# Attention: the softmax scaling on GpSimd, and every second copy of the transposed probabilities on VectorE

## The chip, the cores and the metric

The kernel runs on one core of a Trainium2 chip. The metric is device time in microseconds of one execution. Three runs of the kernel before gave 2448.98, 2449.76 and 2450.52 us, median 2449.76 us.

## The reference

The program is a two-layer decoder trunk on 256 tokens of width 2048. Layer 0 mixes tokens with a diagonal state-space mixer, layer 1 with sparse attention, and each layer ends with a SwiGLU feed-forward part. The change touches only the core of the attention. For each of 16 heads of width 128, and each of two blocks of 128 queries, the reference does, with the 64 keys picked per query by a small indexer:

```
logits = einsum('bqhd,bqkhd->bhqk', qb, kg) * HEAD_DIM ** -0.5
logits = where(valid, logits, -inf)
p      = softmax(logits, axis=-1)
ob     = einsum('bhqk,bqkhd->bqhd', p, vg)
```

The kernel does not gather. It computes the logits against all keys of the block (128 for the first block of queries, 256 for the second) and adds a mask, `selb`, that is zero on the picked keys and very negative elsewhere.

## The kernel before

Each engine has its own program, in which instructions run in the order written; the engines meet at semaphores. Nearly all of the time is TensorE's: matrix products of float32 weights, each split in a high and a low part (line 2217), with the weights streamed from HBM by SyncE through a ring of four slots. ScalarE writes the high part (line 807) and VectorE the low part (line 1155). The weight splitting of the next product and the attention share these two engines one after the other.

The attention stands between the last projection ("v") and the output projection ("z", `attn_out`). Its unit is one head of one block of queries; there are 32, numbered a = 0 to 31. Heads 0 to 15 are *narrow* (128 keys), heads 16 to 31 *wide* (256 keys). Four engines work on them as a pipeline, written out by hand:

- TensorE, function `attention` in its program. Step a issues the logits of head a (line 2154, into `psA` or `psB`), then the transposition of head a-3 (line 2166, out of `prob` into `psT`), then the product of head a-4 with the values (line 2175, out of `probT` into `psM`; four heads fill one bank). The text calls the three L(a), T(a-3) and PV(a-4).
- VectorE. Step a makes the masked logits and their row minimum (line 1647, R(a)), the reciprocal of the row sum of head a-2 (line 1653, I(a-2)), and the scaling of that head's probabilities in place (line 1660, S(a-2)). Once in four steps, ahead of these, it writes the low part of four finished heads (line 1635, `o_lo`).
- ScalarE. Step a copies the transposed probabilities of head a-2 from PSUM to SBUF (line 1030, C(a-2)), then takes the exponential and row sum of head a (line 1036, E(a)), and once in four steps writes the high part of four finished heads (line 1042, `o_hi`).
- GpSimd does nothing in the attention. Its program goes through the same list of runs and, for the norm behind the attention, loads two chunks of layer-norm rows by DMA (line 740), which it issues before the attention begins.

Buffers: `prob` and `logit` have four slots by head modulo 4, `probT` and `psT` two by head modulo 2. The semaphores that order this are `lg_full` (L done), `lg_read` (R done), `exp_done` (E done), `p_ready` (S done), `pT_full` (T done), `pT_ready` (C done), `o_full`, `o_hi` and `o_ready`.

Of the kernel before, what the change touches and what calls it, by code (L numbers as in the profile page):

```python
# [34 lines left out]
P = 128  # L35
# [5 lines left out]
HEADS = 16  # L41
# [63 lines left out]
def build(nc, x, c, positions, ada_w, ada_b, ln_g, ln_b, s5_in_w, s5_a_re, s5_a_im, s5_log_dt, s5_b_re, s5_b_im,  # L105
          s5_c_re, s5_c_im, s5_d, s5_glu_w, s5_glu_b, dsa_in_w, dsa_out_w, ffn_w_in, ffn_w_out, consts, out):
    ctx = ExitStack()
    with ctx:
# [197 lines left out]
        gbias_landed, gate_ready, gate_full, gate_done = sem("gbias_landed"), sem("gate_ready"), sem("gate_full"), sem("gate_done")  # L306
        idx_full, idx_relu, idx_read = sem("idx_full"), sem("idx_relu"), sem("idx_read")
        key_raw, key_turned = sem("key_raw"), sem("key_turned")
        lg_read = sem("lg_read")
        lg_full, lg_ready, exp_done, p_ready, pT_full, pT_ready, o_full, o_hi, o_ready = (  # L310
            sem("lg_full"), sem("lg_ready"), sem("exp_done"), sem("p_ready"), sem("pT_full"), sem("pT_ready"),
            sem("o_full"), sem("o_hi"), sem("o_ready"))
# [402 lines left out]
        @block.gpsimd  # L715
        def _(pool):
            nc.gpsimd.memset(ident[:], 0.0).then_inc(const_ready, 1)
            nc.gpsimd.memset(ones[:].bitcast(F32), 1.0).then_inc(constants, 1)
            pool.wait_ge(const_ready, 1)
            nc.gpsimd.affine_select(out=ident[:], in_=ident[:], compare_op=ALU.not_equal, fill=1.0, base=0,  # L720
                                    pattern=[[-1, P]], channel_multiplier=1).then_inc(constants, 1)
            for ri in range(2):
                nc.gpsimd.memset(Bdiag[ri][:], 0.0).then_inc(constants, 1)

            def load_brow(q):
                chunk0, layer, c0, gate, _ = streamed(q)
                if gate is None:
                    return

                if q:  # L730
                    pool.wait_ge(chunk_stored, q)
                c0 += (q - chunk0) * AW
                pool.dma_start(brow[:], ada_b[layer:layer + 1, c0:c0 + AW].to_broadcast([P, AW])).then_inc(brow_landed, 16)

            def load_rows(norm, chunk):

                if 4 * norm + chunk >= 2:
                    pool.wait_ge(row_used, 4 * norm + chunk - 1)
                for which, src in ((0, ln_g), (1, ln_b)):
                    pool.dma_start(lnrow[:, chunk % 2, which],  # L740
                                   src[norm // 2, norm % 2:norm % 2 + 1, chunk * NB:(chunk + 1) * NB].to_broadcast([P, NB])
                                   ).then_inc(rows_landed[chunk % 2], 16)

            for r in runs:
                if r.before == "ln":
                    if r.norm == 0:
                        pool.wait_ge(w_lo_ready, rounded(r.unit + r.units - 1))
                    if r.norm == 2:
                        pool.wait_ge(idx_full, TOK * IDX_HEADS)
                    for chunk in range(4):  # L750
                        load_rows(r.norm, chunk)
                if r is glu:

                    pool.wait_ge(col_used, FRONT + 1)
                    for j in range(4):
                        pool.dma_start(gate_bias[32 * j:32 * j + 32], ada_b[0:1, 2 * D + j * NB:2 * D + (j + 1) * NB].to_broadcast([32, NB])
                                       ).then_inc(gbias_landed, 16)
                    pool.wait_ge(y_full, len(PIECES))
                if r.kind == "v":

                    pool.wait_ge(T_full, r.turn)
                    nc.gpsimd.memset(causal[:], 1.0).then_inc(const_ready, 1)
                    pool.wait_ge(const_ready, 2)
                    nc.gpsimd.affine_select(out=causal[:], in_=causal[:], compare_op=ALU.is_ge, fill=0.0, base=0,
                                            pattern=[[P, TOK], [-1, SEQ]], channel_multiplier=1).then_inc(constants, 1)
                if r.dense and r is not glu:
                    for q in range(r.dense[0], r.dense[0] + r.dense[1]):
                        load_brow(q)
                    continue
                if not r.ada and r is not glu:  # L770
                    continue
                for i in range(r.n):
                    q = chunk_of(r, i)
                    if r.kind == "glu":

                        pool.wait_ge(ps_free[1], r.use[1] + i)
                        for which, c0 in ((0, D), (1, 0)):
                            pool.dma_start(glub[:, which], s5_glu_b[0:1, c0 + i * NB:c0 + (i + 1) * NB].to_broadcast([P, NB])).then_inc(glub_landed, 16)
                    if q is not None:
                        load_brow(q)  # L780
                if r is glu:
                    for q in range(r.dense[0], r.dense[0] + r.dense[1]):
                        load_brow(q)

            pool.wait_ge(w_used, runs[-1].unit)
            for which, src in ((0, ln_g), (1, ln_b)):
                for chunk in range(4):
                    pool.dma_start(last_row[:, chunk, which],
                                   src[NORMS // 2, NORMS % 2:NORMS % 2 + 1, chunk * NB:(chunk + 1) * NB].to_broadcast([P, NB])
                                   ).then_inc(last_landed, 16)  # L790
# [3 lines left out]
        def _(act):  # L794
# [228 lines left out]
            def attention():  # L1023
                A = TOK * HEADS
                for a in range(A + 3):
                    if 2 <= a < A + 2:
                        b = a - 2
                        N = (b // HEADS + 1) * P
                        act.wait_ge(pT_full, b + 1)
                        nc.scalar.activation(probT[:, b % 2, 0:N], T[:, b % 2, 0:N], ACT.Copy).then_inc(pT_ready, 1)  # L1030
                    if a < A:
                        N = (a // HEADS + 1) * P
                        act.wait_ge(lg_read, a + 1)
                        if a >= 4:
                            act.wait_ge(pT_full, a - 3)
                        nc.scalar.activation(prob[a % 4][:, 0:N], logit[:, a % 4, 0:N], ACT.Exp, bias=soft[:, a % 4, 1:2], scale=-1.0,
                                             accum_out=soft[:, a % 4, 2:3]).then_inc(exp_done, 1)
                    if a >= 6 and a % 4 == 2:
                        g = (a - 6) // 4
                        t, h = divmod(4 * g, HEADS)  # L1040
                        act.wait_ge(o_full, g + 1)
                        nc.scalar.activation(hT_hi[:, h:h + 4, t * P:(t + 1) * P],
                                             M[:, g % 2].rearrange("p (h t) -> p h t", t=P), ACT.Copy).then_inc(o_hi, 1)
# [92 lines left out]
        def _(vec):  # L1136
# [491 lines left out]
            def attention():  # L1628
# [6 lines left out]
                    V.tensor_tensor(hT_lo[:, h:h + 4, t * P:(t + 1) * P], M[:, g % 2].rearrange("p (h t) -> p h t", t=P),  # L1635
                                    hT_hi[:, h:h + 4, t * P:(t + 1) * P].bitcast(F32), ALU.subtract).then_inc(o_ready, 1)

                for a in range(A + 2):
                    if a >= 9 and a % 4 == 1:
                        o_lo((a - 9) // 4)  # L1640
                    if a < A:
                        t = a // HEADS
                        N = (t + 1) * P
                        vec.wait_ge(lg_full, a + 1)
                        if a >= 4:
                            vec.wait_ge(exp_done, a - 3)
                        V.tensor_tensor_reduce(out=logit[:, a % 4, 0:N], in0=PS[a % 2][:, a // 2 % 2, 0:N],
                                               in1=selb[:, t, 0:N], scale=-HD ** -0.5, scalar=3.0e38, op0=ALU.add,
                                               op1=ALU.min, accum_out=soft[:, a % 4, 1:2]).then_inc(lg_read, 1)
                    if a >= 2:  # L1650
                        b = a - 2
                        vec.wait_ge(exp_done, b + 1)
                        V.reciprocal(soft[:, b % 4, 3:4], soft[:, b % 4, 2:3]).then_inc(dve, 1)
                        chain[0] += 1
                        inverse = chain[0]
                    if a >= 2:
                        b = a - 2
                        N = (b // HEADS + 1) * P
                        vec.wait_ge(dve, inverse)
                        V.tensor_scalar(prob[b % 4][:, 0:N], prob[b % 4][:, 0:N], soft[:, b % 4, 3:4], None, ALU.mult  # L1660
                                        ).then_inc(p_ready, 1)
                o_lo(A // 4 - 1)

            def finish(r, i, s):
# [107 lines left out]
        def _(pe):  # L1772
# [369 lines left out]
            def attention():  # L2142
# [14 lines left out]
                for a in range(A + 4):  # L2157
                    if a < A:
                        logits(a)
                    if 3 <= a < A + 3:  # L2160
                        b = a - 3
                        pe.wait_ge(p_ready, b + 1)
                        if b >= 2:
                            pe.wait_ge(pT_ready, b - 1)
                        for k in range(b // HEADS + 1):
                            ins = nc.tensor.transpose(T[:, b % 2, k * P:(k + 1) * P], prob[b % 4][:, k * P:(k + 1) * P], ident[:])
                        ins.then_inc(pT_full, 1)
                    if a >= 4:
                        b = a - 4
                        t, h = divmod(b, HEADS)  # L2170
                        pe.wait_ge(pT_ready, b + 1)
                        if b % 4 == 0 and b >= 8:
                            pe.wait_ge(o_ready, b // 4 - 1)
                        for k in range(t + 1):
# [145 lines left out]
```

## Time and profile before

| | us |
|---|---|
| median of three runs | 2449.76 |
| the profiled execution | 2452.9 |
| its span | 2451.2 |
| TensorE busy | 2391.7 (98% of the span) |
| VectorE busy | 1857.8 (76%) |
| ScalarE busy | 1042.6 (43%) |
| GpSimd busy | 35.3 (1%) |

The profiled execution is one run under the hardware profiler; its span is from the first to the last instruction. Times of rows are from the span's start. The attention runs from about 1580 to 1616 us of it, which is 1.5% of the span. All durations used below come from this execution.

### The profile page before, as it was taken

The numbers are of one execution on the slowest core, as the hardware profiler recorded it, in microseconds if no ns is written. First come the engines' busy times: TensorE is split into PE (matmuls) and PEld (weight loads), VectorE is DVE, ScalarE is ACT, GpSimd is POOL, SyncE is SP. The second block draws the span as 40 slices with busy tenths as digits, with TensorE's granted clock in tenths as the row PEclk, the third lists the DMA queues.
The fourth block names the chain that finished last, engine by engine and source line by source line (L and its number), as shares of the span: only waits on it lengthen the run. The fifth ranks groups of instructions, "written<-read, shape, count | busy, mean of one in ns | idle before, by whom it ended". The sixth has DMA issues, their size and how long they took to land.

```text
span 2451.2 us, 33454 instructions
## 1 busy us (share of the span) xinstructions
PE 2391.7 (98%) x12649; PEld 1923.6 (78%) x12649; DVE 1857.8 (76%) x2994; ACT 1042.6 (43%) x1245; POOL 35.3 (1%) x67
## 2 busy tenths in 40 slices
PE   7997899999999999999999999999999999999998
PEld 5584578878888888888878888778888888888886
DVE  8469969878878887898878987887777754455457
ACT  5353123464434444344454344555544334443442
POOL 0000000000000000000000000000000000000000
PEclk9998999999999999999999999999999999999999
DMA  9978748779989997898758877646788666666674
GB/s 376 398 253 314 285 166 310 248 230 344 311 284 310 341 306 264 292 331 299 254 167 291 290 250 228 203 138 191 254 293 288 220 196 189 189 189 191 195 218 144
DMA packets 311664, 627.39 MB, mean 256 GB/s; under 512 B 26608, under 2 KB 27024, under 8 KB 311504
## 3 DMA queue, kind: packets, MB, share of 16 engines
q1 hardware_dynamic: 306576, 611.27, 73.9%
q0 software_dynamic: 4288, 13.90, 2.0%
q8 instruction: 102, 1.67, 0.3%
q14 instruction: 58, 0.48, 0.1%
q10 hardware_dynamic: 640, 0.08, 0.0%
HBM read 623.05 MB, written 2.10 MB: 255 GB/s over the span
## 4 chain that ended last, share of the span: by engine, by line
PE 94%; DVE 2%; DMA 2%; ACT 1%; issue 1%; SPq 0%; DVEq 0%; ACTq 0%
PE psB L2217 42%; PE psA L2217 41%; DMA col_raw<-in_ada_w 2%; PE psT L1783 1%; PE psM L1815 1%; PE psA L2049 1%; PE psM L1826 1%; PE psT L2030 1%; PE psB L2030 0%; PE psT L1847 0%; PE psT L2019 0%; PE psA L2005 0%; PE psM L1796 0%; PE psM L1795 0%; DMA biasn<-in_ada_b 0%
## 5 line engine op out<-in xcount | busy, mean ns | idle before, releaser
L1155 DVE TENSOR_TENSOR w_lo<-w_raw,w_hi 128x1024 fp32r<-128x1024 f32 x732 | 893.1, 1223 | 465.5 <-ACT w_hi L807 461.0
L807 ACT ACTIVATE w_hi<-w_raw 128x1024 fp32r<-128x1024 f32 x732 | 774.8, 1060 | 1093.5 <-PE psB L2217 497.6
L2217 PE MATMUL psB<-w_hi,hT_hi 128*128 128x512 f32 x1040 | 407.3, 392 | 0.0
L2217 PE MATMUL psB<-w_hi,hT_lo 128*128 128x512 f32 x1040 | 404.9, 389 | 0.0
L2217 PE MATMUL psB<-w_lo,hT_hi 128*128 128x512 f32 x1040 | 404.7, 389 | 0.0
L2217 PE MATMUL psA<-w_hi,hT_hi 128*128 128x512 f32 x1008 | 397.6, 394 | 2.4 <-DVE w_lo L1155 2.1
L2217 PE MATMUL psA<-w_hi,hT_lo 128*128 128x512 f32 x1008 | 392.9, 390 | 0.0
L2217 PE MATMUL psA<-w_lo,hT_hi 128*128 128x512 f32 x1008 | 392.4, 389 | 0.0
L1172 DVE SCALAR_TENSOR_TENSOR ada_acc<-ada_raw,csil,ada_acc 128x512 f32<-128x512 f32 x465 | 347.5, 747 | 14.3 <-DVE ada_acc L1172 0.9
L2217 PEld LDWEIGHTS psB<-w_hi,hT_hi 128*128 128x128 f32 x1040 | 195.2, 188 | 45.9 <-issue 4.5
L2217 PEld LDWEIGHTS psA<-w_hi,hT_hi 128*128 128x128 f32 x1008 | 189.2, 188 | 49.1 <-issue 8.0
L2217 PEld LDWEIGHTS psB<-w_hi,hT_lo 128*128 128x128 f32 x1040 | 195.2, 188 | 40.8
L2217 PEld LDWEIGHTS psB<-w_lo,hT_hi 128*128 128x128 f32 x1040 | 195.3, 188 | 40.0
L2217 PEld LDWEIGHTS psA<-w_hi,hT_lo 128*128 128x128 f32 x1008 | 189.2, 188 | 40.0
L2217 PEld LDWEIGHTS psA<-w_lo,hT_hi 128*128 128x128 f32 x1008 | 189.4, 188 | 37.8
L2217 PE MATMUL psA<-w_hi,aT_hi 128*128 128x512 f32 x448 | 175.0, 391 | 0.8 <-DVE aT_lo L1712 0.7
L2217 PE MATMUL psA<-w_hi,aT_lo 128*128 128x512 f32 x448 | 174.4, 389 | 0.0
L2217 PE MATMUL psA<-w_lo,aT_hi 128*128 128x512 f32 x448 | 174.3, 389 | 0.0
L2217 PE MATMUL psB<-w_hi,aT_hi 128*128 128x512 f32 x432 | 169.1, 391 | 0.0
L2217 PE MATMUL psB<-w_hi,aT_lo 128*128 128x512 f32 x432 | 168.1, 389 | 0.0
L2217 PE MATMUL psB<-w_lo,aT_hi 128*128 128x512 f32 x432 | 168.1, 389 | 0.0
L2217 PEld LDWEIGHTS psA<-w_hi,aT_hi 128*128 128x128 f32 x448 | 84.1, 188 | 18.7 <-issue 1.6
(376 smaller groups left out, 2316.8 us busy)
## 6 DMA issues: line engine op xcount, KB each, us to landing
w_raw<-in_ffn_w_in SPq DMA_DIRECT2D x352, 512.0 KB, 4.6
ada_raw<-in_ada_w SPq DMA_DIRECT2D x496, 256.0 KB, 5.5
w_raw<-in_ffn_w_out SPq DMA_DIRECT2D x176, 512.0 KB, 4.7
col_raw<-in_ada_w SPq DMA_DIRECT2D x128, 512.0 KB, 7.4
w_raw<-in_dsa_in_w SPq DMA_DIRECT2D x112, 512.0 KB, 4.6
w_raw<-in_s_glu_w SPq DMA_DIRECT2D x56, 512.0 KB, 5.7
w_raw<-in_s_in_w SPq DMA_DIRECT2D x32, 512.0 KB, 7.8
w_raw<-in_dsa_out_w SPq DMA_DIRECT2D x32, 512.0 KB, 5.0
```

The costliest lines, as they stand in the source:

```text
L807: nc.scalar.activation(high(u), w_raw[:, u % RING], ACT.Copy).then_inc(w_hi_ready, 1)
L1155: V.tensor_tensor(low(u), w_raw[:, u % RING], high(u).bitcast(F32), ALU.subtract).then_inc(w_lo_ready, 1)
L1172: V.scalar_tensor_tensor(out=ada_sum(q), in0=ada_tile(q, k), scalar=csil[:, k:k + 1], in1=ada_sum(q), op0=ALU.mult, op1=ALU.add).then_inc( ...
L1783: ins = nc.tensor.transpose(T[:, j // 2, (j % 2) * SEQ + t * P:(j % 2) * SEQ + (t + 1) * P], src(t, j), ident[:])
L1815: ins = MM(M[row:row + 32, 0], csil[:, k:k + 1].to_broadcast([P, 32]), col_tile(a + w)[:, b * NB:(b + 1) * NB], start=k == 0, stop=k == AU ...
L1826: ins = MM(M[row:row + 32, v % 2], csil[:, k:k + 1].to_broadcast([P, 32]), col_tile(a + half)[:, b * NB:(b + 1) * NB], start=k == 0, stop= ...
L2030: ins = MM(outputs_place(n, f, d)[rows], Ctab[d][ri][:, f, rows], st[:, c0:c0 + HALF, half, g, ri, f % 8], start=False, stop=f % 4 == 3 an ...
L2049: ins = MM(PS[0][:, t], uT[:, kt, tok], glu_raw[k][:, kk], start=kt == 0, stop=kt == KT - 1)
L2217: ins = MM(PS[s][:, t, 0:r.width], a_[:, kt, tok], b_[:, kk, 0:r.width], start=kt == begin and m == 0, stop=kt == (end or r.units * UK) - ...
```

## The change

The scaling moves from VectorE to GpSimd, which runs it for all 32 heads in order, each behind a new semaphore `inverse_ready` that the reciprocal raises. The loop stands in GpSimd's program at the attention's place, so ahead of the two chunks of layer-norm rows for the norm behind it. ScalarE keeps the copies of even heads. The copies of odd heads move to VectorE, with a semaphore of their own, `pT_other`; VectorE makes the copy of head a-4 at the end of its odd step a, and its loop is two steps longer.

```diff
+                if r.before == "attention":
+                    for b in range(TOK * HEADS):
+                        N = (b // HEADS + 1) * P
+                        pool.wait_ge(inverse_ready, b + 1)
+                        nc.gpsimd.tensor_scalar(prob[b % 4][:, 0:N], prob[b % 4][:, 0:N], soft[:, b % 4, 3:4], None, ALU.mult
+                                                ).then_inc(p_ready, 1)
...
-                    if 2 <= a < A + 2:
+                    if 2 <= a < A + 2 and a % 2 == 0:
                         b = a - 2
                         N = (b // HEADS + 1) * P
                         act.wait_ge(pT_full, b + 1)
...
-                for a in range(A + 2):
+                for a in range(A + 4):
...
-                    if a >= 2:
+                    if 2 <= a < A + 2:
                         b = a - 2
                         vec.wait_ge(exp_done, b + 1)
-                        V.reciprocal(soft[:, b % 4, 3:4], soft[:, b % 4, 2:3]).then_inc(dve, 1)
-                        chain[0] += 1
-                        inverse = chain[0]
-                    if a >= 2:
-                        b = a - 2
+                        V.reciprocal(soft[:, b % 4, 3:4], soft[:, b % 4, 2:3]).then_inc(inverse_ready, 1)
+                    if a >= 4 and a % 2:
+                        b = a - 4
                         N = (b // HEADS + 1) * P
-                        vec.wait_ge(dve, inverse)
-                        V.tensor_scalar(prob[b % 4][:, 0:N], prob[b % 4][:, 0:N], soft[:, b % 4, 3:4], None, ALU.mult
-                                        ).then_inc(p_ready, 1)
+                        vec.wait_ge(pT_full, b + 1)
+                        V.tensor_copy(probT[:, b % 2, 0:N], T[:, b % 2, 0:N]).then_inc(pT_other, 1)
...
-                            pe.wait_ge(pT_ready, b - 1)
+                            pe.wait_ge((pT_ready, pT_other)[b % 2], b // 2)
...
-                        pe.wait_ge(pT_ready, b + 1)
+                        pe.wait_ge((pT_ready, pT_other)[b % 2], b // 2 + 1)
```

## Rows read from the trace of the kernel before

**Rows 1.** Stretches of the span: length; us busy of PE, PEld, DVE, ACT, POOL, granted TensorE clock, DMA share, GB/s.
```profile
1580.40:1593.30 12.90, 10.04 (x70) 8.42 (x71) 10.78 (x62) 10.39 (x44) 0.00 (x0) 1.00 0.32 114
1593.30:1616.00 22.70, 21.40 (x142) 16.48 (x141) 17.69 (x77) 17.50 (x61) 0.00 (x0) 1.00 0.00 1
1616.00:1650.00 34.00, 34.00 (x151) 28.11 (x151) 28.52 (x32) 14.28 (x14) 0.00 (x0) 1.00 0.66 217
```

**Rows 2.** Chain of waits, narrow heads: start us, us on the chain, what.
```profile
1585.07 0.29 DVE logit L1647
...
1585.51 0.30 DVE prob L1660
1585.85 0.33 PE psT L2166
...
1586.66 0.29 DVE logit L1647
```

**Rows 3.** TensorE in order of time, narrow heads: start us, us, line, operation, operands.
```profile
1586.02 0.39 PE L2175 MATMUL psM<-probT,v 128*128 128x128 f32 x2
1586.24 0.39 PE L2154 MATMUL psA<-qkT 128*128 128x128 f32 x2
1586.46 0.32 PE L2166 MATMUL psT<-ident,prob 128*128 128x128 f32 x1
...
1589.36 0.32 PE L2166 MATMUL psT<-ident,prob 128*128 128x128 f32 x1
...
1592.86 0.32 PE L2166 MATMUL psT<-ident,prob 128*128 128x128 f32 x1
```

**Rows 4.** TensorE in order of time, wide heads.
```profile
1596.51 0.60 PE L2154 MATMUL psB<-qkT 128*128 128x256 f32 x2
...
1601.14 0.60 PE L2154 MATMUL psB<-qkT 128*128 128x256 f32 x2
1601.57 0.38 PE L2166 MATMUL psT<-ident,prob 128*128 128x128 f32 x2
1601.79 0.61 PE L2175 MATMUL psM<-probT,v 128*128 128x128 f32 x4
1602.24 0.60 PE L2154 MATMUL psA<-qkT 128*128 128x256 f32 x2
...
1606.38 0.38 PE L2166 MATMUL psT<-ident,prob 128*128 128x128 f32 x2
```

**Rows 5.** VectorE in order of time, one low part and one wide head.
```profile
1587.39 0.69 DVE L1635 TENSOR_TENSOR hT_lo<-psM,hT_hi 128x512 fp32r<-128x512 f32 x1
1588.00 0.28 DVE L1647 CUSTOM_DVE_ANT_0 logit<-psB,selb 128x128 f32<-128x128 f32 x1
...
1597.14 0.42 DVE L1647 CUSTOM_DVE_ANT_0 logit<-psB,selb 128x256 f32<-128x256 f32 x1 [0.27 <-PE psB L2154]
...
1597.49 0.16 DVE L1653 RECIPROCAL soft<-soft 128x1 f32<-128x1 f32 x1
1597.69 0.35 DVE L1660 TENSOR_SCALAR prob<-prob,soft 128x256 f32<-128x256 f32 x1
```

**Rows 6.** VectorE groups by shape: a copy out of PSUM, count, busy us, mean ns.
```profile
L1516 DVE COPY st<-psM 128x512 f32<-128x512 f32 x4 | 2.6, 688 | 1.4 <-PE psM L2005 1.4
```

**Rows 7.** GpSimd in order of time: its computing instructions.
```profile
1.24 0.29 POOL L720 TENSOR_SCALAR_AFFINE_SELECT ident<-ident 128x128 f32<-128x128 f32 x1
1.48 1.79 POOL L723 MEMSET Bdiag_re<- 128x2048 f32 x1
...
1493.64 0.62 POOL L764 TENSOR_SCALAR_AFFINE_SELECT causal<-causal 128x512 f32<-128x512 f32 x1
```

**Rows 8.** All engines in order of time: GpSimd woken by VectorE.
```profile
1797.11 0.68 DVE L1188 SCALAR_TENSOR_TENSOR grow<-psM,brow 128x512 f32<-128x512 f32 x1
...
1798.09 0.54 POOL L733 DMA_DIRECT2D brow<-in_ada_b  x1 [52.38 <-DVE grow L1188]
```

**Rows 9.** A stretch with a lower granted clock, columns as in rows 1.
```profile
220.00:230.00 10.00, 5.04 (x32) 0.83 (x32) 10.00 (x65) 0.00 (x0) 0.00 (x0) 0.76 1.02 411
```

More of the change, by code:

```diff
@@ L308, in build @@
         key_raw, key_turned = sem("key_raw"), sem("key_turned")
-        lg_read = sem("lg_read")
+        lg_read, inverse_ready, pT_other = sem("lg_read"), sem("inverse_ready"), sem("pT_other")
         lg_full, lg_ready, exp_done, p_ready, pT_full, pT_ready, o_full, o_hi, o_ready = (
```

## The prediction

> **What bounds the kernel now.** I read the table of stretches first. Behind the attention TensorE is busy for the whole of the stretch [rows 1], so what the attention gives or takes moves the end of the span one for one: no later stage waits on something else that could absorb it. In the attention itself TensorE is busy 10.04 of 12.90 us with narrow heads and 21.40 of 22.70 us with wide ones [rows 1]. The reader is to see that there is little to win with wide heads and a little more with narrow ones.
>
> Then I read the chain of waits in the narrow part. It goes round once in two heads: R(a) at 1585.07, S(a-2) 0.44 later, T(a-2) 0.34 after that, L(a+2) 0.39 after T, and R(a+2) 0.42 after L, which is 1585.07 to 1586.66, 1.59 us [rows 2, 3]. Once in four heads o_lo holds VectorE for 0.61 us [rows 5], and four heads take 3.50 us (1589.36 to 1592.86) [rows 3]. Wide heads take 4.81 us for four (1601.57 to 1606.38) [rows 4].
>
> **The pieces that I use**, start to start. Narrow: L 0.22 [rows 3]; T 0.17 (1585.85 to 1586.02) and PV 0.22 [rows 2, 3]; L to R 0.42; R to I 0.24 (0.44 less the 0.20 from I to S in the wide rows) [rows 2, 3, 5]. Wide: L 0.43, T 0.22, PV 0.45 [rows 4]; L to R 0.63 (1596.51 to 1597.14), R to I 0.35, I to the next instruction 0.20 [rows 4, 5]. An instruction's end to its waiter's start costs 0.05: the scaling lasts 0.29 and T starts 0.34 after it [rows 2].
>
> **The change part by part.**
>
> *The scaling off VectorE.* Removed: 32 instructions that took 0.21 to 0.28 of VectorE's line. On the chain above I to T was 0.20 + 0.34 = 0.54. It becomes the reciprocal's 0.16 [rows 5] plus X, X being the way into GpSimd, the multiplication there, and the way to TensorE. No row shows this multiplication on GpSimd. The nearest is its select of the same kind (one tensor in, one out): 0.29 for 128 columns and 0.62 for 512, so about 0.40 for 256 [rows 7]. The longest computing row is 1.79 [rows 7]. The way in is 0.05 at the least, and 0.30 by the row in which a VectorE result (ends 1797.79) releases a DMA issue at 1798.09 [rows 8]. I take the select: X = 0.05 + 0.29 + 0.05 = 0.39 narrow and 0.50 wide. The lower end is the same less a third. For the upper end I take 1.79 for wide and half, 0.90, for narrow, with 0.30 on the way in: X = 1.25 and 2.14.
>
> GpSimd's select took 0.33 us for 384 more columns, 0.86 ns each [rows 7]. The Trainium skill, "GPSIMD Engine Reference", section 3.1, speaks against this part of the change: elementwise work belongs on VectorE, since GpSimd needs about 2.6 cycles of 1.2 GHz per element. By that the multiplication would be, as an estimate, 0.28 and 0.55 plus the dispatch, and X some 0.1 to 0.3 larger than mine; the sum below would be the same, as the limits on X there show. The trace has the one-input select well under that rate; for the multiplication itself no row decides.
>
> *The copy of odd heads to VectorE.* This is where I see the cost. VectorE makes C(a-4) at the end of its odd step a, behind R(a) and I(a-2). R(a) needs L(a). TensorE issues L(a), T(a-3) and then PV(a-4), which needs this very copy. So PV(a-4) cannot start until L(a) has gone through VectorE, and everything of TensorE queues behind PV(a-4): L(a+1) and T(a-2) above all. ScalarE's copy was made right after T(a-4), some two steps earlier. The copy reads PSUM: 128x512 took 0.69 [rows 6]; R, which also reads PSUM, took 0.28 for 128 and 0.42 for 256 [rows 5]; I take 0.29 and 0.42, the bounds being the scaling's 0.35 and the copy's 0.69, worth -0.07 and +0.27 a pair.
>
> A pair of narrow heads, a odd, from L(a) = 0: R 0.42, I 0.66, copy 0.86, PV(a-4) 0.86 + 0.29 + 0.05 = 1.20, L(a+1) 1.42, T(a-2) 1.64, PV(a-3) 1.81 (ScalarE's copy was done long before), L(a+2) 2.03. Against it, once in four heads: I(a-1) falls at 1.42 + 0.42 + 0.24 = 2.08, o_lo at 2.28, and R(a+2) at 2.89 where it was due at 2.45, so 0.44 more. Four heads: 2 x 2.03 + 0.44 = 4.50 against 3.50.
>
> A pair of wide heads: R 0.63, I 0.98, copy 1.18, PV(a-4) 1.65, L(a+1) 2.10, T(a-2) 2.53, PV(a-3) 2.75, L(a+2) 3.20. o_lo ends at 3.28 + 0.61 = 3.89 where R(a+2) was due at 3.83: 0.06. Four heads: 6.46 against 4.81.
>
> *Is X covered?* T(a-1) follows L(a+2) and stands just ahead of PV(a-2), which cannot start before 2.03 + 1.20 = 3.23. T may start as late as 3.06 and cost nothing; its reciprocal ends at 2.08 + 0.16 = 2.24. So X is free up to 0.82 narrow. Wide: 3.20 + 1.65 - 0.22 = 4.63, less 3.24, so up to 1.39. My 0.39 and 0.50 are covered by the wait for the copy. Without that cover a pair costs 1.21 + X narrow, 1.81 + X wide (the loop of rows 2 with X in it).
>
> *The copy off ScalarE.* Sixteen copies fewer. ScalarE is not the last to arrive any more, so this is worth nothing.
>
> *The moved loads.* Four DMA issues of GpSimd for layer-norm rows go behind its 32 multiplications. The norm is beyond the 34 us of products shown [rows 1], an issue took 0.54 [rows 8], so nothing waits. If they were late, it would cost about 2 us.
>
> **The sum.** Start of the pipeline, the first transposition through GpSimd with nothing to hide it: 0.2. Heads 4 to 16, twelve narrow steps: 3 x 1.00 = 3.0. Heads 16 to 20, logits wide and copies narrow, the mean of the two: (1.00 + 1.65) / 2 = 1.3. Heads 20 to 31, eleven steps of 1.65 / 4 = 0.41: 4.5. The tail behind L(31): the last o_lo but one, I(31), C(29) and then C(31) follow each other on VectorE, where S(31) alone was late: about 0.9, with an error of as much. Together 9.9 us. The profiled execution would go from 2452.9 to 2462.8; the median of the runs is 3.1 below it, so 2449.8 + 9.9 = 2459.7.
>
> **Rivals.**
>
> *GpSimd is dear.* Same mechanism, but X beyond the limits, so T and not PV comes last. With the upper end: narrow 2.46 a pair against 1.75, six pairs, 4.3; wide 3.95 against 2.41, seven and a half pairs, 11.6; start and tail 1.1. Together 17.0, 2466.8. For it: no row shows the operation. Against: three compute rows of GpSimd at under 1 ns a column.
>
> *Relief wins (faster).* VectorE's line is the busiest after TensorE's, o_lo's 0.61 shows on the chain, and it loses 0.2 to 0.3 a head. If the copies of odd heads came early enough, TensorE would go at its own pace: narrow 0.61 a head, 3.50 - 2.44 = 1.06 in four, times 3; wide 1.10 a head, 4.81 - 4.40 = 0.41 in four, times 3.75. That is 3.2 + 1.5 = 4.7, 2445.1. The point that decides is whether C(a-4) starts before L(a) does; by the order written it starts 0.86 after. Only if TensorE ran L(a) well ahead of PV(a-4), against that order, would it be so.
>
> *It evens out.* The added wait is as long as the time that VectorE's line is freed by, the multiplications saved giving back the rest: 2450. For it: the cost falls on every second head only. Against: the pair comes to 2.03 against 1.75 with VectorE's relief already in it.
>
> *The clock falls.* Where TensorE was busy 5.04 of 10 us the granted clock was 0.76 [rows 9], the mean of 2.4 and 1.2 GHz; at 10.04 of 12.90 it stayed at 1.00 [rows 1]. After the change the narrow part has 1.22 us of issues in 2.25. If the clock fell to 1.2 GHz through four wide pairs, about 2.0 of TensorE's work on each pair's loop would double, 8 us, and some 2 us more at the start of the products: 9.9 + 10 = 2469.7. Against: the gaps stay under 1 us.
>
> **How the numbers follow.** The forecast as worked out, 2457 to 2462, has 0.68. Dear GpSimd, 2462 to 2467 or above, 0.15. The clock 0.04. Relief 0.07. Evening out 0.06. About 0.2%, 4.9 us, is what a measurement of this kernel can tell from no change. Slower by more is 0.68 + 0.15 + 0.04 = 0.87, within 0.06, faster 0.07: relief's 4.7 is at the edge, and I count it as faster. The range is 2456.5 to 2467.0: it takes in the dear end of X, and the cheap end of the copy together with a tail that costs nothing; the clock, relief and evening out stay outside.
>
> **What would show it.** In the changed trace the chain of waits should pass from L to R, I and the new copy on VectorE and from there to PV, in every odd head. TensorE should idle before PV of odd heads by about 0.8 us narrow and 1.0 wide, put down to VectorE's `probT`, and hardly before T. Four heads should take 4.5 and 6.5 us, and the attention 45 us where it took 35. GpSimd's multiplication should last 0.3 to 0.6. I am wrong if TensorE's idle time stands before T and names GpSimd's `prob`, if GpSimd's instructions take over 0.8, or if PV of odd heads starts less than 1 us after L of four heads on.

## The result, and the profile after

The changed kernel takes 2461.38 us (median of 6 runs, 2460.27 to 2461.85) against 2450.03 us for the kernel before (6 runs): 11.35 us more, ratio 1.0044, 95% interval [1.0034, 1.0054]. It is slower, by 9.9 us in the forecast and by 11.35 in the measurement, and inside the range of 2456.5 to 2467.0.

The two profiled spans differ by less, 2459.5 against 2451.2 us. The attention began at 1577.05 in the one and at 1580.38 in the other, although all that had changed ahead of it were four DMA issues of GpSimd for layer-norm rows, which now come behind it; the profiled execution of the kernel before had lost some 3 us earlier on. Had the moved loads won these 3 us, the medians would differ by some 8 us and not by 11.35. So from here on the measure is the *length* of the attention, from the first logits to the first product behind it: 35.37 us before (1580.38 to 1615.75), 46.85 us after (1577.05 to 1623.90), 11.48 more.

The table of stretches, after (narrow heads, wide heads, the products behind; columns as in [rows 1]):

```profile
1577.05:1594.97 17.92, 13.17 (x69) 10.59 (x70) 8.65 (x56) 9.42 (x38) 8.23 (x14) 0.81 0.23 79
1594.97:1623.90 28.93, 23.30 (x141) 16.82 (x140) 14.46 (x65) 14.59 (x51) 17.54 (x22) 1.00 0.01 2
1623.90:1658.00 34.10, 34.10 (x153) 28.25 (x152) 28.23 (x32) 14.28 (x14) 0.66 (x2) 1.00 0.74 246
```

VectorE's busy time in the narrow part fell from 10.78 to 8.65 us and ScalarE's from 10.39 to 9.42 [rows 1], and yet the part is 5 us longer: work was taken from engines, and time was added between them. Behind the attention TensorE is busy throughout, as before, so the delay stays. The third number to read is the clock, 0.81 in the narrow part where it had been 1.00.

TensorE in order of time, wide heads of the changed kernel, the counterpart of [rows 4]:

```profile
1608.17 0.60 PE L2157 MATMUL psB<-qkT 128*128 128x256 f32 x2
1609.29 0.44 PE L2169 MATMUL psT<-ident,prob 128*128 128x128 f32 x2 [0.52 <-POOL prob L763]
1609.69 0.71 PE L2178 MATMUL psM<-probT,v 128*128 128x128 f32 x4
1610.24 0.60 PE L2157 MATMUL psA<-qkT 128*128 128x256 f32 x2
1610.67 0.38 PE L2169 MATMUL psT<-ident,prob 128*128 128x128 f32 x2
1610.89 0.61 PE L2178 MATMUL psM<-probT,v 128*128 128x128 f32 x4
1611.34 0.60 PE L2157 MATMUL psB<-qkT 128*128 128x256 f32 x2
```

A pair takes 3.17 us (L at 1608.17 to L at 1611.34), where 3.20 was forecast. PV of the odd head starts 1.52 after L (1608.17 to 1609.69), 1.65 was forecast. VectorE and GpSimd between the two, the counterparts of [rows 5] and [rows 7]:

```profile
1608.81 0.42 DVE L1653 CUSTOM_DVE_ANT_0 logit<-psB,selb 128x256 f32<-128x256 f32 x1
...
1609.15 0.16 DVE L1659 RECIPROCAL soft<-soft 128x1 f32<-128x1 f32 x1
1609.23 0.41 DVE L1664 COPY probT<-psT 128x256 f32<-128x256 f32 x1
```

```profile
1596.21 0.60 POOL L763 TENSOR_SCALAR prob<-prob,soft 128x128 f32<-128x128 f32 x1 [1.10 <-DVE soft L1659]
...
1608.31 0.92 POOL L763 TENSOR_SCALAR prob<-prob,soft 128x256 f32<-128x256 f32 x1 [1.14 <-DVE soft L1659]
```

The copy ends at 1609.64 and PV starts 0.05 later. GpSimd's multiplication ends at 1609.23 and T starts at 1609.29. From T to PV it takes 0.27 when T comes after a wait and PV does not (1600.01 to 1600.28), so by T alone PV could have gone at 1609.56: the copy is last, by 0.13 us. Multiplications take 0.60 and 0.92, where the nearest rows of GpSimd had suggested 0.29 and 0.40.

The waits of the attention, after (engine, tile and line, for whom: us in all, times, longest):

```profile
PEld psT L2169 <- POOL prob L763: 14.6, 19, 1.7
PE psT L2169 <- POOL prob L763: 9.0, 14, 1.5
PEld psM L2178 <- DVE probT L1664: 4.0, 13, 0.7
PE psM L2178 <- DVE probT L1664: 0.9, 3, 0.5
```

Most of these waits carry GpSimd's name, and so does the chain of waits (the counterpart of [rows 2]):

```profile
1607.71 0.31 DVE logit L1653
1608.06 0.08 DVE soft L1653
1608.14 0.09 DVE soft L1659
1608.23 0.08 issue
1608.31 0.93 POOL prob L763
1609.24 0.04 issue
1609.29 0.44 PE psT L2169 x2
1609.72 0.68 PE psM L2178 x4
1610.40 0.45 PE psA L2157 x2
```

Read alone, this chain says that GpSimd is the cause. The ends of two waits lie 0.13 us apart here, and the profile shows TensorE idle only before the first of them. Which one counts is for the experiments.

Stretch by stretch, from one transposition to another, before and after, in us:

| | before | after | more |
|---|---|---|---|
| first L to T(0) | 2.28 | 2.67 | 0.39 |
| T(0) to T(4) | 3.19 | 5.11 | 1.92 |
| T(4) to T(8) | 3.51 | 5.12 | 1.61 |
| T(8) to T(12) | 3.50 | 4.63 | 1.13 |
| T(12) to T(16) | 4.08 | 5.43 | 1.35 |
| T(16) to T(20) | 4.63 | 6.11 | 1.48 |
| T(20) to T(24) | 4.81 | 6.33 | 1.52 |
| T(24) to T(28) | 4.82 | 6.34 | 1.52 |
| T(28) to the product | 4.55 | 5.11 | 0.56 |

### The profile page after: what moved, and what is told of

Same layout as the page of the kernel before. It is cut to its first block, busy times and chain, and to the rows that moved or that the text cites. A ratio compares the mean times of both kernels' runs of the same rounds, so it can differ in the third digit from the quotient of the medians.

```text
span 2459.5 us, 33454 instructions
## 1 busy us (share of the span) xinstructions
PE 2396.7 (97%) x12649; PEld 1926.0 (78%) x12649; DVE 1852.3 (75%) x2978; ACT 1038.6 (42%) x1229; POOL 59.6 (2%) x99
## 4 chain that ended last, share of the span: by engine, by line
PE 88%; DVE 8%; DMA 1%; ACT 1%; issue 1%; POOL 0%; SPq 0%; DVEq 0%; ACTq 0%
PE psB L2220 41%; PE psA L2220 39%; DVE prod L1497 2%; DVE tmp L1502 1%; DVE st L1508 1%; PE psT L1786 1%; PE psM L1818 1%; DVE w_lo L1161 1%; DMA w_raw<-in_dsa_out_w 0%; DMA w_raw<-in_s_in_w 0%; PE psA L2052 0%; POOL prob L763 0%; PE psM L2178 0%; PE psT L1850 0%; PE psT L2033 0%
```

## The experiments

Two theories. *A*: VectorE's late copy holds PV of odd heads behind L, R and I of the same step, and GpSimd is hidden behind that. *B*: GpSimd's multiplication, late into TensorE, sets the time. *C* is about the clock and comes last. Results first, as a map ("narrow" is T(8) to T(12), "wide" T(20) to T(24); low clock is the time at 1.2 GHz by the granted clock in 2 us stretches):

| kernel | length | narrow | wide | low clock | median of the runs |
|---|---|---|---|---|---|
| before | 35.37 | 3.50 | 4.81 | none | 2450.0 |
| the change | 46.85 | 4.63 | 6.33 | 6.8 | 2461.4 |
| e1 scaling alone | 42.29 | 3.93 | 5.87 | none | 2457.5 |
| e2 late copy alone | 53.84 | 6.68 | 7.44 | 13.6 | 2472.1 |
| e3 change, copy early | 43.45 | 4.17 | 5.87 | 3.4 | 2458.9 |
| e4 change, half of GpSimd's columns | 45.71 | 4.48 | 6.33 | 6.8 | 2460.4 |
| e5 before, one step deeper | 32.05 | 3.05 | 4.40 | 3.4 | 2446.1 |
| e6 early copy alone | 38.41 | 3.70 | 5.14 | 3.4 | 2452.4 |
| e7 change, idle stretch filled | 46.04 | 5.12 | 6.34 | 3.4 | 2460.5 |
| e8 change, early and deeper | 33.75 | 3.26 | 4.39 | 3.4 | 2449.0 |
| e9 change, late and deeper | 44.79 | 4.51 | 6.33 | 6.8 | 2459.4 |

In e2 the whole narrow stretch, and in e7 1.5 us of it, lie at the low clock, so these two figures are not to be compared with the rest of their column. The kernel before, run beside them, had medians of 2450.64 us with e1 to e4, 2450.95 with e5 to e8 and 2450.98 with e9.

### e1: the scaling on GpSimd alone

```diff
 (in the changed kernel)
-                    if 2 <= a < A + 2 and a % 2 == 0:
+                    if 2 <= a < A + 2:
 ...
-                    if a >= 4 and a % 2:
-                        b = a - 4
-                        ...
-                        V.tensor_copy(probT[:, b % 2, 0:N], T[:, b % 2, 0:N]).then_inc(pT_other, 1)
 ...
-                        pe.wait_ge((pT_ready, pT_other)[b % 2], b // 2 + 1)
+                        pe.wait_ge(pT_ready, b + 1)
```

> The scaling on GpSimd alone; ScalarE makes all copies. Length of the attention, from the first logits to the first product behind it: 35.4 us before, 46.9 after the whole change. Theory A (the late copy on VectorE holds PV of odd heads, and GpSimd's 0.60 and 0.92 us are mostly hidden behind it): without that copy nothing hides GpSimd, a pair costs 1.21 + 0.73 = 1.94 narrow and 1.81 + 1.06 = 2.87 wide against 1.75 and 2.41, so about 6 us over before: length 41.5, time 2456. Theory B (GpSimd's multiplication sets the time, the copy matters little): the whole cost stays, length 46 to 47, time 2461.

Length 42.29, median 2457.54 us, ratio 1.0029 [1.0018, 1.0039]. Theory A's 41.5 is near, B's 46 to 47 is not. The chain of waits, wide heads:

```profile
1605.51 0.45 PE psA L2152 x2
1605.96 0.02 issue
1605.98 0.06 DVE logit L1653
1606.04 0.29 issue
1606.33 0.08 DVE soft L1653
1606.41 0.09 DVE soft L1659
1606.50 0.08 issue
1606.58 0.93 POOL prob L763
1607.51 0.04 issue
1607.56 0.44 PE psT L2164 x2
```

Here the loop really runs L, R, I, multiplication, T, and a pair costs 2.93 us (5.87 / 2), where 1.81 + X with X = 1.06 gave 2.87. GpSimd by itself costs 6.9 us of length (42.29 against 35.37). It is shorter than the change's 6.33 for four wide heads, so this loop is not what bounds the change.

### e2: the late copy alone

```diff
 (in the changed kernel; the loop on GpSimd is gone)
-                        V.reciprocal(soft[:, b % 4, 3:4], soft[:, b % 4, 2:3]).then_inc(inverse_ready, 1)
+                        V.reciprocal(soft[:, b % 4, 3:4], soft[:, b % 4, 2:3]).then_inc(dve, 1)
+                        ...
+                        V.tensor_scalar(prob[b % 4][:, 0:N], prob[b % 4][:, 0:N], soft[:, b % 4, 3:4], None, ALU.mult
+                                        ).then_inc(p_ready, 1)
```

> The odd copies on VectorE alone, at the same place; the scaling stays on VectorE between reciprocal and copy. Theory A: the copy now stands behind R, I and S, 0.12 (narrow) to 0.25 us (wide) and the wait between I and S later than in the whole change; about 14 us over before, more than the whole change: length 49, time 2463 to 2464. Theory B: near before, length 36 to 37, time 2451.

Length 53.84, median 2472.09 us, ratio 1.0085 [1.0070, 1.0100]. With no work on GpSimd at all it is the slowest of all: B falls here. Theory A has the sign, but its length of 49 is too small by 5 us and its time by 8. Part of this is the clock: 13.6 us at 1.2 GHz are in its profile. As 3.4 us of them cost 0.7 to 0.8 us in two pairs of profiles below, 13.6 would be worth some 3, an estimate; the rest stays open.

### e3: the change with the copy one step earlier

```diff
-                    if a >= 4 and a % 2:
-                        b = a - 4
+                    if 4 <= a < A + 4 and a % 2 == 0:
+                        b = a - 3
```

> The whole change with VectorE's copy of an odd head one step earlier, at the end of step a-1, so ahead of R(a) and its wait for L(a). Theory A: PV no longer waits for the copy, what is left is the loop through GpSimd, about 7 us over before: length 42.5, time 2457, and TensorE waits for GpSimd's prob alone. Theory B: no change against the whole change, length 46 to 47, time 2461.

Length 43.45, median 2458.85 us, ratio 1.0031 [1.0020, 1.0043], a little over what A said. Wide heads take 5.87 for four, as in e1: with the copy out of the way, what is left is the loop through GpSimd. So the early copy by itself gives back only 3.4 of the 11.5 us; the second loop stands close behind the first.

### e4: GpSimd scales half the columns

Half of each head's probabilities stays unscaled.

```diff
-                        N = (b // HEADS + 1) * P
+                        N = (b // HEADS + 1) * P // 2
                         pool.wait_ge(inverse_ready, b + 1)
```

> The whole change with GpSimd scaling only the first half of each head's columns (the other half stays unscaled), so about 0.45 us narrow and 0.60 wide. Theory A: T moves earlier but PV does not, at most 0.1 us a pair narrow and nothing wide: length 45 to 46, time 2460. Theory B: 0.15 us a pair narrow and 0.32 wide come back, with a little at the ends 3.5 to 4 us: length 43, time 2457.5.

Length 45.71, median 2460.38 us, ratio 1.0038 [1.0025, 1.0051]. TensorE, wide heads:

```profile
1607.98 0.60 PE L2157 MATMUL psB<-qkT 128*128 128x256 f32 x2
1608.78 0.44 PE L2169 MATMUL psT<-ident,prob 128*128 128x128 f32 x2 [0.20 <-POOL prob L763]
1609.50 0.71 PE L2178 MATMUL psM<-probT,v 128*128 128x128 f32 x4 [0.28 <-DVE probT L1664]
```

The multiplication fell from 0.92 to 0.60 us, and the wait before T from 0.52 to 0.20, exactly as much. The 0.32 us come back as a wait of 0.28 before PV; PV is 1.52 after L as before, and four wide heads take 6.33 as before. The wait that the profile put down to GpSimd was worth nothing in the wide part. In the narrow part it was worth 0.15 in four heads (4.63 to 4.48), and over the whole attention 1.14 us (46.85 to 45.71), within what A allowed and far from B's 43.

### e9 and e8: the loop through GpSimd spread over three heads

Both are the changed kernel with one step more between the logits and the rest: TensorE transposes head a-4 and multiplies head a-5 at step a, and ScalarE's copies, o_hi and o_lo follow one step later. They differ in VectorE's copy alone:

```diff
 (TensorE, in both)
-                    if 3 <= a < A + 3:
-                        b = a - 3
+                    if 4 <= a < A + 4:
+                        b = a - 4
 ...
-                    if a >= 4:
-                        b = a - 4
+                    if a >= 5:
+                        b = a - 5
 (VectorE's copy, e8)
+                    if a >= 5 and a % 2:
+                        b = a - 4
 (VectorE's copy, e9)
+                    if a >= 6 and a % 2 == 0:
+                        b = a - 5
```

> As e8_deep_both, but VectorE's copy behind R(a) and I(a-2) of the step in which TensorE needs it, as in the change; the loop through GpSimd stays spread over three heads. Theory A: PV of odd heads waits again for L(a), R(a), I(a-2) and the copy, 1.04 to 1.10 us narrow and about 1.5 wide behind L(a): 8 to 9 us over e8, length 41.5 to 42.5, time 2456 to 2458. Theory B (only the loop through GpSimd mattered, the place of the copy does not): as e8, length 34, time 2449.

> The whole change (scaling on GpSimd, odd copies on VectorE) with one step more between logits and transposition, and the copies ahead of R(a). Theory A: the loop through GpSimd is spread over three heads, 1.94 / 3 = 0.65 and 2.87 / 3 = 0.96 a head, below TensorE's own 1.10 for wide heads; nothing of the change's cost is left and 2 to 3 us are won over before: length 32.5 to 33.5, time 2447.5 to 2448.5. Theory B (GpSimd is too slow for its share, 0.93 us a wide head): length above 38.

e9: length 44.79, median 2459.38 us, ratio 1.0036 [1.0021, 1.0050]. Its length is 2.3 us over the upper end of what A said, with 6.8 us at 1.2 GHz in it. TensorE, wide heads:

```profile
1604.86 0.60 PE L2157 MATMUL psA<-qkT 128*128 128x256 f32 x2
1605.30 0.38 PE L2169 MATMUL psT<-ident,prob 128*128 128x128 f32 x2
1606.38 0.71 PE L2178 MATMUL psM<-probT,v 128*128 128x128 f32 x4 [0.70 <-DVE probT L1664]
1606.93 0.60 PE L2157 MATMUL psB<-qkT 128*128 128x256 f32 x2
```

T does not wait at all in these heads now, GpSimd is out of the picture there, and PV starts 1.52 us after L once more. Four wide heads take 6.33, the same as the change; the 2.06 us of length between e9 and the change lie elsewhere. e8, where only the copy's place is another, takes 4.39: 1.94 us in four heads for one line's position. Its length is 33.75 and its median 2449.04 us, ratio 0.9992 [0.9983, 1.0001], which cannot be told from the kernel before; A had said 32.5 to 33.5, and 2 to 3 us under the kernel before, which the medians do not show. The same instructions on the same engines as in the change cost nothing against the kernel before, though e5, with the same depth and neither part of the change, is 1.70 us shorter still.

### e6: the early copy alone

e2 with the copy placed as in e3.

> Scaling on VectorE as before; VectorE makes the odd copies at the end of step a-1, ahead of R(a). Against e2 (the same copies one half step later, length 53.8) it moves only the place. Theory A: the place was the cost: about 1.5 to 2.5 us over before, from the copy's own 0.2 to 0.35 us on VectorE: length 37 to 38, time 2452 to 2453. Rival (VectorE simply has too much work with the copies): length above 45.

Length 38.41, median 2452.35 us, ratio 1.0005 [0.9996, 1.0014], within 0.5 us of A's upper end of 38 and far from the rival's 45. From e2 to e6, 15.4 us of length go with the copy's place; VectorE has the same work in both.

### e5: the kernel before, one step deeper

```diff
 (in the kernel before; ScalarE, then TensorE)
-                    if 2 <= a < A + 2:
-                        b = a - 2
+                    if 3 <= a < A + 3:
+                        b = a - 3
 ...
-                    if 3 <= a < A + 3:
-                        b = a - 3
+                    if 4 <= a < A + 4:
+                        b = a - 4
 ...
```

PV, o_hi and o_lo follow one step later as well.

> The kernel before with one step more between the logits and the rest: TensorE transposes head a-4 and multiplies head a-5 at step a, ScalarE copies head a-3; nothing on GpSimd, no copy on VectorE. Theory A (the attention before and after the change is bound by loops of latencies: L, R, I, S, T, and back to L two heads later): the loop is spread over three heads, and the engines' own work is left, 0.77 narrow (VectorE) and 1.10 wide (TensorE) a head against 0.875 and 1.20, so 3 to 4.5 us less than before: length 31 to 32.5, time 2446 to 2447.5. Rival: VectorE or ScalarE is already the bound and a longer pipeline only lengthens the tail: length 35.5 to 36.5, time 2450 to 2451.

Length 32.05, median 2446.10 us, ratio 0.9979 [0.9970, 0.9988]: 4.9 us faster than the kernel before, and the fastest of all. Its chain of waits, wide heads, stays on TensorE, which is the bound there:

```profile
1600.07 0.43 PE psB L2154 x2
1600.50 0.22 PE psT L2166 x2
1600.72 0.45 PE psM L2175 x4
1601.17 0.43 PE psA L2154 x2
```

1.10 us a head is TensorE's own time, and 4.40 in four heads is what was measured. So the kernel before was held by a loop of latencies over two heads, and not by an engine. The scaling on GpSimd put more latency into that loop (e1). The late copy made a second one beside it, from L(a) to PV(a-4) within one step of TensorE, and that one a deeper pipeline does not loosen (e9).

### e7, e10 and e11: the clock

The granted clock in the changed kernel's first microseconds (columns as in [rows 1]):

```profile
1578.00:1579.00 1.00, 0.18 (x2) 0.00 (x0) 0.66 (x8) 0.99 (x5) 0.00 (x0) 1.00 0.87 262
1579.00:1580.00 1.00, 0.28 (x2) 0.28 (x3) 0.32 (x3) 0.14 (x2) 0.94 (x2) 0.76 0.95 356
1580.00:1581.00 1.00, 1.00 (x6) 0.92 (x6) 0.34 (x3) 0.76 (x4) 0.25 (x1) 0.50 0.95 367
...
1586.00:1587.00 1.00, 1.00 (x8) 0.91 (x7) 0.42 (x4) 0.78 (x2) 0.00 (x0) 0.83 0.02 8
```

0.50 is 1.2 GHz. Theory C: the idle stretch of 1.54 us before the first transposition, longer than before by 0.39, brought it on. e7 fills it:

```diff
                     if a < A:
                         logits(a)
+                    if a == 3:
+                        for _ in range(7):
+                            MM(M[:, 1, 0:P], ident[:], ident[:], start=True, stop=True)
```

> The whole change with seven products of the identity with itself (128x128, about 0.22 us each, into a bank of psM that the first later products overwrite) between the first four logits and the first transposition, where TensorE sat idle for 1.5 us. Theory C (that idle stretch lets the clock fall to 1.2 GHz for the 6.5 us behind it, and this costs 1.5 us or more of the 46.9): the granted clock stays at 1.00, length 45 to 45.5, time 2459.5 to 2460. Rival (the clock does not hang on this stretch, since the same stretch stood at full clock with the scaling alone on GpSimd): the clock falls all the same in this or another place, length 46 to 47, time 2461.

Length 46.04, median 2460.51 us, ratio 1.0039 [1.0025, 1.0053]. The seven products fill the stretch from 1577.92 to 1579.63, and T(0) comes 2.68 after the first logits, as in the change. The clock still fell, later (1586.6 to 1590.0) and for 3.4 us. e1 had the same start as the change, T(0) 2.67 after the first logits, and kept 1.00. Two unchanged kernels were profiled again:

> The kernel before, profiled once more. Theory C (only kernels with longer idle stretches of TensorE lose the clock in the attention): granted clock 1.00 through the attention, length 35.4. Rival (it is a matter of the single execution): 0.95 or less in the attention and a length of 36 to 37.

> The changed kernel, profiled once more. Theory C: the clock falls again at the start of the attention, length 46 to 47. Rival: the clock falls elsewhere or not at all, and the length differs with it, 45 to 46 at full clock.

The kernel before, second profile: length 36.04, and a low clock that its first profile had not shown:

```profile
1582.00:1584.00 2.00, 2.00 (x10) 1.95 (x11) 1.32 (x8) 1.52 (x8) 0.00 (x0) 0.53 0.55 212
1584.00:1586.00 2.00, 2.00 (x12) 1.83 (x10) 1.27 (x8) 1.18 (x6) 0.00 (x0) 0.61 0.00 0
```

The changed kernel, second profile: length 46.85, the clock low again, from about 1578.6 to 1585.5. So C falls as stated: the low clock comes in the attention of the kernel before as well, in some executions. What differs is how long it lasts, 3.4 us there and 6.8 in the change, and e7's single profile does not settle why. What starts it was not found.

## Why the prediction was right, and where it was off

**Nothing behind absorbs it.** Right: TensorE is busy 34.10 of 34.10 us behind the attention, and 11.48 us of length are 11.35 us of median.

**The copy holds PV of odd heads.** Right for wide heads, and shown from three sides: e2 has the late copy without GpSimd, e4 halves GpSimd's time and the wide heads do not move, e9 takes GpSimd out of the loop and keeps 6.33. Forecast were 4.50 and 6.46 us for four heads, measured 4.63 and 6.33. The wide ones are cheaper since the copy follows the reciprocal by 0.08 us and not 0.20: the 0.20 was the distance to an instruction that had to wait for the reciprocal's result, and the copy does not need it.

For narrow heads the copy shares the place with GpSimd. In a pair without a low part PV could go by the copy at 1590.00, 0.05 behind its end; it goes at 1590.11, as T allows, and T waited for GpSimd:

```profile
1589.68 0.27 DVE L1664 COPY probT<-psT 128x128 f32<-128x128 f32 x1
...
1589.95 0.33 PE L2169 MATMUL psT<-ident,prob 128*128 128x128 f32 x1 [0.60 <-POOL prob L763]
1590.11 0.39 PE L2178 MATMUL psM<-probT,v 128*128 128x128 f32 x2
```

In the next pair the copy is last again, because VectorE writes a low part first and has to wait 0.32 us for ScalarE's high part, a wait that the forecast had left out:

```profile
1591.49 0.69 DVE L1641 TENSOR_TENSOR hT_lo<-psM,hT_hi 128x512 fp32r<-128x512 f32 x1 [0.32 <-ACT hT_hi L1048]
```

So the 4.63 beside a forecast of 4.50 is in part luck: the copy came 0.12 us a pair earlier than forecast, and these two waits went the other way.

**X, the way through GpSimd.** The size was off. 0.39 and 0.50 were forecast; measured are 0.08 + 0.60 + 0.05 = 0.73 and 0.08 + 0.92 + 0.06 = 1.06. It cost little because X is covered, but less well than I wrote: with the faster copy the limits of 0.82 and 1.39 shrink by 0.12 and 0.13 to 0.70 and 1.26. The wide X is under its limit, the narrow one just over it, and e4 got 0.15 back in four narrow heads. The rule of the Trainium skill that I set beside it ("GPSIMD Engine Reference", section 3.1, about 2.6 cycles of 1.2 GHz per element) was nearer than the select: 0.32 us for 128 more columns is 2.5 ns, 3.0 cycles, each. The section ties its figure to an operation with two inputs; this one has one tensor and a scalar per partition.

**The sum, term by term.** In the forecast's own steps, counted by the logits of TensorE:

| term | forecast | before | after | more |
|---|---|---|---|---|
| start, L(0) to L(4) | 0.2 | 2.44 | 2.94 | 0.50 |
| narrow, L(4) to L(16) | 3.0 | 10.44 | 14.98 | 4.54 |
| mixed, L(16) to L(20) | 1.3 | 4.16 | 5.54 | 1.38 |
| wide, L(20) to L(31) | 4.5 | 13.34 | 17.16 | 3.82 |
| tail, L(31) to the product | 0.9 | 4.99 | 6.23 | 1.24 |
| together | 9.9 | 35.37 | 46.85 | 11.48 |

The term that was mis-sized is the narrow one. Its first four steps, L(4) to L(8), took 5.98 us against 3.41, and they lie in the 6.8 us at 1.2 GHz (1579.5 to 1586.4). In e7, with 3.4 us at 1.2 GHz in place of 6.8, the twelve steps took 14.25, 0.73 less. In the second profile of the kernel before, 3.4 us at 1.2 GHz where the first had none, they took 11.12, 0.68 more. By these two, as an estimate, the 6.8 us are worth about 1.4, and without them the twelve steps would be some 3.1 over before, where 3.0 was forecast. I had the clock as a rival on its own, with 0.04, at full weight through the wide heads; it came in small, in nearly every profile, beside the main cause. The start and the tail were each 0.3 too small, the wide term 0.7 too large, so that the sum is nearer to the measurement than its parts, and in this there is luck.

**ScalarE's relief** shows nowhere as a gain, as said, though no run has it alone. **The moved loads** were issued from 1622.37 on and nobody waited for them.

**What would show it.** Wrong in one point that matters for reading. I wrote that TensorE would idle before PV and hardly before T, and that GpSimd's name there would mean that I was wrong. GpSimd's name stands there, with 9.0 us against 0.9. With X at 1.06 in place of 0.50 the wait before T became visible, and as TensorE is in order, T's wait came first and left little of PV's. With wide heads it was still PV's that decided. A second sign fired too: GpSimd's instructions take 0.92 with wide heads, over the 0.8 that was to show me wrong. The tests in the forecast were bad ones; e4 is the good one.

**The rivals.** Relief (faster) and evening out fall with the change's own time. Dear GpSimd came true as to GpSimd's price and not as to its effect.

## What to carry to other kernels

When an engine that works in order gets an instruction for another engine, look at what stands ahead of it in the same step and what that waits for: here one line's place was worth 1.94 us in four heads, with the same work on every engine (e8 and e9). How much it is worth depends on the loop behind it: in the change itself moving the line gave back 3.4 of 11.5 us (e3), and loosening the loop through GpSimd 2.1 (e9), but both together gave 13.1 (e8). A profile names the wait that an engine meets first, and if two end close together, only shortening one of them tells which counts. Where no engine is full and the chain comes back to its start after two units of work, one more step of distance between the stages can be worth more than moving work: alone it gave the kernel before 4.9 us (e5). It does nothing for a wait that begins and ends within one step, as that of the late copy.

## What the runs showed of the hardware

A multiplication by a per-partition scalar on GpSimd, in place in SBUF, takes 0.60 us for 128 columns and 0.92 for 256, twice the 0.29 and about 0.40 of its select instruction. It starts 0.08 us after VectorE's result and TensorE follows it by 0.05. In eleven of thirteen profiles the granted clock fell to 1.2 GHz for 3.4 to 13.6 us within the attention, and 3.4 us of it cost 0.7 to 0.8 us of length (36.04 against 35.37, 46.85 against 46.04); of two profiles of the kernel before one shows it and one does not.
